# Hand-over from attention to output mix in a decoder layer: chunk 0's rows of the 16-step pattern by DMA from SBUF to SBUF, eight DRAM stores moved behind them

## The chip, the cores and the metric

One Trainium2 chip, one of its cores. The metric is the device time of one execution of the whole layer in microseconds (us); lower is better.

## The reference

One decoder layer over 2048 tokens of width 1024. What bears on the change is the attention group: eight heads of 64, three dilated window patterns, joined by their softmax denominators.

```python
DILATED_PATTERNS = ((128, 1), (512, 4), (2048, 16))
def dilated_attention_branch(q, k, v, pos):
    q, k = apply_rotary(q, pos, inv_freq), apply_rotary(k, pos, inv_freq)
    for window, dilation in DILATED_PATTERNS:
        o, lse = dilated_pattern(q, k, v, window, dilation)
        outs.append(o); lses.append(lse)
    w = jax.nn.softmax(jnp.stack(lses, axis=0), axis=0)
    return jnp.sum(w[..., None] * jnp.stack(outs, axis=0), axis=0)

def reference(...):
    h = rms_norm(x, g_pre_mix)
    rq, rk, rv, rg, aq, ak, av = split(h @ w_in)
    ret = retention_branch(rq, rk, rv, rg)          # chunks of 128 tokens, a state from chunk to chunk
    att = dilated_attention_branch(aq, ak, av)
    x = x + rms_norm(concatenate([ret, att]) @ w_out, g_post_mix)
    h = rms_norm(x, g_pre_ffn)
    return x + rms_norm((silu(h @ w_gate) * (h @ w_up)) @ w_down, g_post_ffn)
```

All tensors are float32. In the pattern with dilation 16 the token t belongs to class t mod 16, and each class is one block of 128 queries.

## The kernel before, in words

The program has three stages. `project` makes the projections. `attention` handles the heads in pairs, four **units** (NU = 4), and in each unit 48 **blocks** of 128 queries (NB = 48): blocks 0 to 15 of dilation 1, 16 to 31 of dilation 4, 32 to 47 of dilation 16. The last stage is one block of code in which `mix` (retention, joining of the three patterns, output projection, both norms) runs over 16 chunks of 128 tokens, and `ffn` follows it. Between `attention` and the last stage every engine meets at a barrier: none starts the new stage before all have ended the old one, SyncE (SP) too.

In `attention` VectorE scores and copies, ScalarE takes exponentials, TensorE multiplies and transposes. Four blocks make a **quad**. The result of a block is a row tile `orow[:, j % 16, :]`, 128 queries by 132 numbers: two sums, 2 x 64 output columns, two minima. VectorE's copy on line 853 (`copy_out`) ends a quad and raises `o_copied`. SP then stores each block to `att_out` in DRAM (line 715, 66 KB), with one semaphore of `stored` for each of the 16 places in the ring. DRAM is there because of the regrouping: the tokens of a block of dilation 16 lie 16 apart, and `mix` wants 128 successive tokens with all three patterns in one tile, `att_in[s]`, 128 tokens by 3 patterns by 4 units of 132 numbers.

SP's order is written out by hand. In the last unit, `sync` on line 718 ff. stores blocks 0 to 43 as they come, and between them `early_sync` issues loads that `mix` needs first; at block 32 it waits on the 16 `stored` semaphores for what the first three units stored, and loads columns 0 to 395 of `att_in[0]` (line 1170). The last four stores stand at the head of the next stage's SP program (`store_last`), followed by two small constants (line 1206), a wait on the 16 semaphores for all stores, and then:

```python
sp.dma_start(att_in[0][:, :, LAST_UNIT:], att_rows(0)[:, :, LAST_UNIT:]).then_inc(att_loaded[0], 16)   # L1209
load_att(sp, 1, 1)                                                                                # L1143
```

In `mix`, chunk 0 runs so. TensorE turns k (line 1298) and scores (line 1306), VectorE applies decays (lines 1386, 1392), TensorE multiplies (lines 1268, 1272) and forms the chunk's key-value products (line 1282, semaphore `kv_done`). VectorE, after the decays, waits for `att_in[0]` in `lowest_parts` (line 1361), forms the weights of the patterns (to line 1380; ScalarE's exponential on line 1489 in between), masks the key-value products (line 1400, which also waits for `kv_done`), sums a variance (lines 1410, 1412), makes the scores of chunk 1, adds the three weighted parts, and scales the retention output (line 1439). TensorE then turns chunk 0 (line 1250), goes through chunk 1's products, and begins the first dense matmuls of the output projection (line 1345). GpSimd (POOL) weights the parts (line 1539) and takes the roots. The same tile's second copy, `att_in[1]`, is read by VectorE for chunk 1 at its second visit to line 1361.

Of the kernel before, what the change touches and what calls it, by code (L numbers as in the profile page):

```python
# [14 lines left out]
P = 128  # L15
# [17 lines left out]
PATTERNS = (1, 4, 16)  # L33
# [613 lines left out]
def attention(nc, D, bank, first, mixed):  # L647
# [5 lines left out]
    NB = len(blocks)  # L653
# [62 lines left out]

    def store_last(sp):

        for j in range(NB - QUAD, NB):
            store_copied(sp, NU - 1, j)  # L720

    def sync(sp):
        def store(u, j):
            sp.wait_ge(o_copied, NB // QUAD * u + j // QUAD + 1)
            store_copied(sp, u, j)

        def unit(u, s, more=True):

            sp.wait_ge(permuted, BY_16 * u + C_PERMUTED)
            sp.sem_inc(waited, 1)  # L730
            sp.wait_ge(scored, NB * u + C_SCORED)
            sp.sem_inc(waited, 1)
            for j in range(NB):
                if more or j < NB - QUAD:
                    store(u, j)
                if more:
                    for n in range(2 * QK_DMAS):
                        if (n // 2 if n < QK_DMAS else QK_DMAS // 2 + 5 * (n - QK_DMAS) // 2) == j:
                            load_qk(sp, D, first, u + 1, 1 - s, n)
                if more and j and j % 4 == 0:  # L740
                    load_values(sp, D, first, u + 1, j // 4 - 1)
                if not more:
                    mixed["early_sync"](sp, j, permuted, BY_16 * NU + C_PERMUTED, [(sem, 16 * ((NU - 1) * NB // RING) + 16) for sem in stored])
            if more:
                load_values(sp, D, first, u + 1, VALUE_LOADS - 1)

        for r, free in enumerate(first["row_free"]):
            sp.wait_ge(free, first["rows_stored"])
        with sp.Fori(0, NU // 2 - 1) as it:
            unit(2 * it, 0)  # L750
            unit(2 * it + 1, 1)
        unit(NU - 2, 0)
        unit(NU - 1, 1, more=False)

# [172 lines left out]
    with nc.Block() as block:  # L927
# [18 lines left out]
        def _(pool):  # L946
            gpsimd(pool)
            mixed["early_gpsimd"](pool)
    mixed["store_last"] = store_last
    mixed["rows_stored"] = [(sem, 16 * (NU * NB // RING) + 16) for sem in stored]  # L950
    spent = [sem for sem in m.given if sem not in stored]
    return spent + [consts, qk_first, qk_rest] + v_loaded + first["row_free"]
# [13 lines left out]
def mix(nc, D, ident, bank):  # L966
# [61 lines left out]
             "h2_done h_turned h_copied").split()  # L1028
    S = {n: m.sem(n) for n in names}
    qkv_loaded, att_loaded = m.sems("qkv_loaded", 2), m.sems("att_loaded", 2)  # L1030
    x_loaded = m.sems("x_loaded", 2)
    x1_stored, h_stored = m.sem("x1_stored"), m.sem("h_stored")
    late_consts, gains_loaded, w_loaded = m.sem("late_consts"), m.sem("gains_loaded"), m.sem("w_loaded")
# [105 lines left out]
    def att_rows(c):  # L1139
        return D["att_out"][:, bass.ts(c, P), :].rearrange("a t n -> t a n")  # L1140
# [5 lines left out]
        src = D["projT"][RG:RG + WIDTH, bass.ts(c, P)].rearrange("(k p) t -> p k t", p=P)  # L1146
        sp.dma_start(gate[:, s], src).then_inc(att_loaded[s], 16)

    def early_sync(sp, j, permuted, all_permuted, rows_stored):

        if j in (1, 4, 7, 10):
            k = 2 * (j // 3)
# [14 lines left out]
        if j == 32:  # L1167
            for sem, count in rows_stored:
                sp.wait_ge(sem, count)
            sp.dma_start(att_in[0][:, :, 0:LAST_UNIT], att_rows(0)[:, :, 0:LAST_UNIT]).then_inc(S["consts"], 16)  # L1170

    def early_vector(dve, j, permuted, all_permuted):

# [25 lines left out]
    def sync(sp, fed):  # L1199
# [1 line left out]

            sp.sem_inc(S["waited"], 1)

        bounds["store_last"](sp)
        for tile, name in ((head_cols, "head_cols"), (chunk_decay, "chunk_decay")):
            sp.dma_start(tile[:], D[name]).then_inc(late_consts, 16)
        for sem, count in bounds["rows_stored"]:
            sp.wait_ge(sem, count)
        sp.dma_start(att_in[0][:, :, LAST_UNIT:], att_rows(0)[:, :, LAST_UNIT:]).then_inc(att_loaded[0], 16)  # L1209
        load_att(sp, 1, 1)  # L1210
        sp.dma_start(gain_mix[:], D["g_post_mix"].broadcast_to([P, DM])).then_inc(gains_loaded, 16)
        sp.dma_start(gain_ffn[:], D["g_pre_ffn"].broadcast_to([P, DM])).then_inc(gains_loaded, 16)
# [139 lines left out]
    def vector(dve, fed):  # L1352
        dve.wait_ge(S["consts"], 16 * CONSTS)

        def step(c, s, on):
            def lowest_parts():
                a = att_in[s][:].rearrange("p a (u n) -> p a u n", n=AO_W)
                lowest = a[:, :, :, 2 * (ATT_D + 1):AO_W]
                three = lambda t: t[:].rearrange("p a (u h) -> p a u h", h=2)
                wait_loaded(dve, att_loaded[s], c, s, 2)  # L1360
                nc.vector.tensor_reduce(att_low[:].rearrange("p (u h) -> p u h", h=2), lowest.rearrange("p a u h -> p u h a"),
                                        AX.X, ALU.min).then_inc(S["maxed"], 1)
                dve.wait_ge(S["maxed"], c + 1)
                if later(c):
                    dve.wait_ge(S["parted"], 3 * c)
                least = att_low[:].rearrange("p (u h) -> p u h", h=2).unsqueeze(1).broadcast_to([P, 3, 4, 2])
                nc.vector.tensor_tensor(three(weight), lowest, least, ALU.subtract).then_inc(S["differed"], 1)
# [146 lines left out]
    def gpsimd(pool):  # L1514
# [6 lines left out]
        def step(c, s, on):  # L1521
# [31 lines left out]
        steps(pool, step)  # L1553

    bounds.update({"sync": sync, "tensor": tensor, "vector": vector, "scalar": scalar, "gpsimd": gpsimd, "sems": S, "early_gpsimd": early_gpsimd,
            "early_sync": early_sync, "early_vector": early_vector, "store_x1": store_x1, "store_h": store_h, "turn_h": turn_h, "make_x1": make_x1, "make_h2": make_h2,
            "square_y": square_y, "square_x": square_x, "copy_h": copy_h, "root_y": root_y, "root_x": root_x,
            "x1_stored": x1_stored, "h_stored": h_stored})
    return bounds
# [1076 lines left out]
```

## Time and profile before

| | |
|---|---|
| runs | 2401.86, 2406.1, 2407.64 us; median 2406.1 |
| profiled execution | 2404.06 us, its span 2402.2 us |
| TensorE busy | 2352.5 us, 98% of the span |
| VectorE, ScalarE, GpSimd busy | 62%, 38%, 25% |
| mean granted TensorE clock | 0.994 of full |

Times below are microseconds from the span's start. A row of the timeline gives start, duration, engine, line, operation, output and input tiles, how many instructions are merged into it, and in brackets how long the engine stood idle before it and what ended that. SPq are SP's instructions that issue DMAs; their duration is that of the issue, not of the transfer. Matmul ends are modelled, so neighbouring rows can overlap a little. A merged row ends at its start plus its duration.

### The profile page before, as it was taken

How to read it: one execution, taken by the hardware profiler on the slowest of the kernel's cores; microseconds unless marked ns; L12 is line 12 of the kernel's file. 1: busy time of each engine (PE TensorE's matmuls, PEld its weight loads, DVE VectorE, ACT ScalarE, POOL GpSimd, SP SyncE). 2: the span in 40 equal slices, each digit the busy share in tenths (PEclk: the TensorE clock that was granted, in tenths of full speed). 3: DMA queues.
4: the chain of work that ended last, by engine and by line, in shares of the span. 5: the costliest groups of instructions: out<-in, count | busy, mean ns of one | idle time of the engine just before them, and what ended most of it. 6: DMA issues, size and time to landing. Idle time of an engine off the chain costs nothing. (4 is left out here: it accounts for less than half of the span.)

```text
span 2402.2 us, 36587 instructions
## 1 busy us (share of the span) xinstructions
PE 2352.5 (98%) x12624; PEld 1968.4 (82%) x12624; DVE 1484.5 (62%) x2769; ACT 917.2 (38%) x1982; POOL 597.7 (25%) x387
## 2 busy tenths in 40 slices
PE   7999999999999899999999999999999999999998
PEld 6888888888889778887888888878888888888887
DVE  4322346645888878789765666876565654456655
ACT  4301122216878623335433333533333343323332
POOL 0089555535544556662000000000000000000001
PEclk9999999999999989999999999999999999999999
DMA  5323214457777555665433333343333336445655
GB/s 180 126 83 110 75 61 122 130 141 183 186 178 195 165 176 183 187 187 197 144 109 92 105 96 115 117 136 101 107 109 93 103 121 219 145 154 193 232 197 191
DMA packets 309294, 344.96 MB, mean 144 GB/s; under 512 B 17088, under 2 KB 240704, under 8 KB 308928
## 3 DMA queue, kind: packets, MB, share of 16 engines
q1 hardware_dynamic: 309184, 343.54, 46.9%
q8 instruction: 63, 1.03, 0.2%
q14 instruction: 47, 0.39, 0.1%
HBM read 231.41 MB, written 112.07 MB: 143 GB/s over the span
## 5 line engine op out<-in xcount | busy, mean ns | idle before, releaser
L1874 PE MATMUL fin_psum_bank<-ff_b_hi,ff_w_hi 128*128 128x512 f32 x1232 | 481.4, 391 | 8.1 <-ACT ff_taken L2015 5.0
L1874 PE MATMUL fin_psum_bank<-ff_b_lo,ff_w_hi 128*128 128x512 f32 x1232 | 479.9, 390 | 0.0
L1874 PE MATMUL fin_psum_bank<-ff_b_hi,ff_w_lo 128*128 128x512 f32 x1232 | 479.8, 389 | 0.0
L2193 POOL TENSOR_TENSOR ff_ssq<-ff_ssq,ff_minus_half 128x1 f32<-128x1 f32 x16 | 14.8, 928 | 1247.5 <-DVE ff_ssq L2485 1247.5
L1874 PEld LDWEIGHTS fin_psum_bank<-ff_b_hi,ff_w_hi 128*128 128x128 f32 x1232 | 231.6, 188 | 60.2 <-ACT ff_taken L2015 7.0
L1874 PEld LDWEIGHTS fin_psum_bank<-ff_b_hi,ff_w_lo 128*128 128x128 f32 x1232 | 231.6, 188 | 48.4
L1874 PEld LDWEIGHTS fin_psum_bank<-ff_b_lo,ff_w_hi 128*128 128x128 f32 x1232 | 231.7, 188 | 47.5
L1956 PE MATMUL fin_psum_bank<-ff_down_hi,ff_act_hi 128*128 128x512 f32 x616 | 239.8, 389 | 0.5 <-DVE ff_act_lo L2225 0.5
L1956 PE MATMUL fin_psum_bank<-ff_down_hi,ff_act_lo 128*128 128x512 f32 x616 | 239.6, 389 | 0.0
L1956 PE MATMUL fin_psum_bank<-ff_down_lo,ff_act_hi 128*128 128x512 f32 x616 | 239.6, 389 | 0.0
L2197 DVE TENSOR_TENSOR ff_w_lo<-ff_raw,ff_w_hi 128x512 fp32r<-128x512 f32 x176 | 120.8, 687 | 140.2 <-ACT ff_w_hi L1967 140.2
L460 PE MATMUL pr_psum_acc<-pr_hT_hi,pr_w_hi 128*128 128x512 f32 x512 | 199.2, 389 | 0.0
L460 PE MATMUL pr_psum_acc<-pr_hT_lo,pr_w_hi 128*128 128x512 f32 x512 | 199.2, 389 | 0.0
L460 PE MATMUL pr_psum_acc<-pr_hT_hi,pr_w_lo 128*128 128x512 f32 x512 | 199.2, 389 | 0.0
L894 ACT ACTIVATE at_prob<-at_prob,at_orow 128x256 f32<-128x256 f32 (+1 forms) x384 | 173.0, 453 | 56.1 <-DVE at_orow L865 55.5
L2015 ACT ACTIVATE ff_taken<-fin_psum_bank 128x512 f32<-128x512 f32 x132 | 78.8, 597 | 222.9 <-PE fin_psum_bank L1874 219.7
L1987 ACT ACTIVATE ff_act_hi<-ff_act_raw 128x1408 fp32r<-128x1408 f32 x56 | 77.4, 1381 | 204.2 <-DMA ff_act_raw<-a_parts 204.1
L1967 ACT ACTIVATE ff_w_hi<-ff_raw 128x512 fp32r<-128x512 f32 x176 | 109.7, 626 | 105.9 <-PE fin_psum_bank L1874 100.3
L2197 DVE TENSOR_TENSOR ff_w_lo<-ff_sums,ff_w_hi 128x512 fp32r<-128x512 f32 x132 | 90.3, 689 | 88.8 <-ACT ff_w_hi L1967 88.8
L865 DVE CUSTOM_DVE_ANT_0 at_prob<-fin_psum_bank,mask 128x256 f32<-128x256 f32 (+1 forms) x384 | 117.2, 359 | 36.4 <-PE fin_psum_bank L777 34.6
L2225 DVE TENSOR_TENSOR ff_act_lo<-ff_act_raw,ff_act_hi 128x1408 fp32r<-128x1408 f32 x56 | 90.9, 1623 | 75.1 <-ACT ff_act_hi L1987 74.5
L1956 PEld LDWEIGHTS fin_psum_bank<-ff_down_hi,ff_act_hi 128*128 128x128 f32 x616 | 115.6, 188 | 24.8 <-DVE ff_act_lo L2225 0.9
(212 smaller groups left out, 4630.5 us busy)
## 6 DMA issues: line engine op xcount, KB each, us to landing
ff_act_raw<-a_parts SPq DMA_DIRECT2D x56, 704.0 KB, 4.1
ff_raw<-in_w_gate SPq DMA_DIRECT2D x22, 1024.0 KB, 5.9
ff_raw<-in_w_up SPq DMA_DIRECT2D x22, 1024.0 KB, 5.3
a_parts<-ff_a_sum SPq DMA_DIRECT2D x88, 256.0 KB, 6.0
ff_down_raw<-in_w_down SPq DMA_DIRECT2D x77, 256.0 KB, 4.6
a_parts<-ff_up SPq DMA_DIRECT2D x66, 256.0 KB, 2.3
att_out<-at_orow SPq DMA_DIRECT2D x192, 66.0 KB, 3.7
vblk<-v_att SPq DMA_DIRECT2D x48, 256.0 KB, 4.8
```

What stands on the lines that cost most here:

```text
L460: last = nc.tensor.matmul(acc[:, g, :], w[s][:, k, :], h[:, k, t], start=k == 0 and n == 0, stop=k == KT - 1 and n == 2)
L865: last = nc.vector.tensor_tensor_reduce(out=prob[:, n % 4, h, keys[j]], in0=s_ps[:, n % NS, h, keys[j]], in1=mask[:, keys[j]], scale=-SCAL ...
L894: last = nc.scalar.activation(pr, pr, ACT.Exp, bias=orow[:, n % RING, LEAST + h:LEAST + h + 1], scale=-1.0, accum_out=orow[:, n % RING, SU ...
L1874: last = nc.tensor.matmul(to, w[:, i, k, :], b[i][:, k, :], start=fresh and k == 0 and which == 0, stop=k == KH - 1 and which == 2, skip_g ...
L1956: last = nc.tensor.matmul(bank[:, ORDER[n], :], a[t % 3][:, k, :], w[o % 2][k][:], start=k == 0 and which == 0, stop=k == PAIRS - 1 and wh ...
L1967: nc.scalar.activation(w_hi[:, i], weight(i, s), ACT.Copy).then_inc(w_hi_done[i], 1)
L1987: nc.scalar.activation(act_hi[t % 3][:], act_raw[t % 3][:], ACT.Copy).then_inc(act_hi_done, 1)
L2015: nc.scalar.activation(taken[:, i, :], X[s], ACT.Copy).then_inc(snapped, 1)
L2193: nc.gpsimd.tensor_tensor(ssq[:, n % 2, 1:2], ssq[:, n % 2, 1:2], minus_half[:], ALU.pow).then_inc(rooted, 1)
L2197: nc.vector.tensor_tensor(w_lo[:, i], weight(i, s), w_hi[:, i].bitcast(F32), ALU.subtract).then_inc(w_lo_done[i], 1)
L2225: nc.vector.tensor_tensor(act_lo[t % 3][:], act_raw[t % 3][:], act_hi[t % 3][:].bitcast(F32), ALU.subtract).then_inc(act_lo_done, 1)
```

## The change

For the last unit alone, the 16 blocks of dilation 16 get a second way out. The tokens of chunk 0 are the first eight rows of each of these row tiles, and SP sends them straight to `att_in[0]` by a DMA from SBUF to SBUF, 8 rows of 132 numbers (4 KB), to every 16th partition. Twelve of these stand in the attention's SP program behind the stores of blocks 32 to 43's places, four at the head of the next stage. The other two patterns of chunk 0's last unit are loaded from DRAM at block 38, after a wait on the 16 `stored` semaphores for blocks 0 to 31. The DRAM stores of blocks 40 to 43 leave the attention's program; eight stores, blocks 40 to 47, now stand in the next stage behind the straight ones and the two constants. The load on line 1209 is gone. VectorE waits once more, for `far_loaded`.

```diff
     def store_last(sp):
 
+        for j in range(NB - 2 * QUAD, NB):
+            store_copied(sp, NU - 1, j)
+
+    def straight(sp, j):
+        far = PATTERNS[-1]
+        mixed["far_rows"](sp, j - (NB - far), far, orow[0:P // far, j % RING, :])
+
+    def straight_last(sp):
         for j in range(NB - QUAD, NB):
-            store_copied(sp, NU - 1, j)
+            straight(sp, j)
...
-                if more or j < NB - QUAD:
+                if more or j < NB - 2 * QUAD:
                     store(u, j)
+                elif j < NB - QUAD:
+                    sp.wait_ge(o_copied, NB // QUAD * u + j // QUAD + 1)
...
                 if not more:
-                    mixed["early_sync"](sp, j, permuted, BY_16 * NU + C_PERMUTED, [(sem, 16 * ((NU - 1) * NB // RING) + 16) for sem in stored])
+                    if NB - PATTERNS[-1] <= j < NB - QUAD:
+                        straight(sp, j)
+                    mixed["early_sync"](sp, j, permuted, BY_16 * NU + C_PERMUTED,
+                                        *([(sem, 16 * (NU * NB // RING - back) + 16) for sem in stored] for back in (3, 1)))
...
+    def far_rows(sp, r, far, rows):
+        sp.dma_start(att_in[0][r:P:far, 2, LAST_UNIT:], rows).then_inc(far_loaded, 16)
...
+        if j == 38:
+            for sem, count in near_stored:
+                sp.wait_ge(sem, count)
+            sp.dma_start(att_in[0][:, 0:2, LAST_UNIT:], att_rows(0)[:, 0:2, LAST_UNIT:]).then_inc(att_loaded[0], 16)
...
-        bounds["store_last"](sp)
+        bounds["straight_last"](sp)
         for tile, name in ((head_cols, "head_cols"), (chunk_decay, "chunk_decay")):
             sp.dma_start(tile[:], D[name]).then_inc(late_consts, 16)
+        bounds["store_last"](sp)
         for sem, count in bounds["rows_stored"]:
             sp.wait_ge(sem, count)
-        sp.dma_start(att_in[0][:, :, LAST_UNIT:], att_rows(0)[:, :, LAST_UNIT:]).then_inc(att_loaded[0], 16)
         load_att(sp, 1, 1)
...
                 wait_loaded(dve, att_loaded[s], c, s, 2)
+                if not later(c):
+                    dve.wait_ge(far_loaded, 16 * PATTERNS[-1])
```

SP's program around the end of the attention, before. The branches are the end of the attention's code and the way into the next stage, the barrier between them; `x11` means eleven in a row:

```order
L1170 DMA mx_att_in_3172<-att_out 128x3x396
L715 DMA att_out<-at_orow 128x132 x11
L927 UNCONDITIONAL_BRANCH
L2565 UNCONDITIONAL_BRANCH
L715 DMA att_out<-at_orow 128x132 x4
L1206 DMA mx_head_cols<-const_head_cols 128x256
L1206 DMA mx_chunk_decay<-const_chunk_decay 128x2
L1209 DMA mx_att_in_3172<-att_out 128x3x132
L1143 DMA mx_att_in_3173<-att_out 128x3x528
```

The same engine and place after the change, the part ahead of the barrier from block 36 on (blocks 32 to 35 alternate in the same way; block 32's straight DMA stands just ahead of the load of 128x3x396):

```order
L1164 DMA mx_att_in_3172<-at_orow 8x132
L715 DMA att_out<-at_orow 128x132
L1164 DMA mx_att_in_3172<-at_orow 8x132
L1191 DMA mx_att_in_3172<-att_out 128x2x132
L715 DMA att_out<-at_orow 128x132
L1164 DMA mx_att_in_3172<-at_orow 8x132 x5
L940 UNCONDITIONAL_BRANCH
L2588 UNCONDITIONAL_BRANCH
```

Between the load at block 32 and the barrier SP issued 11 DMAs, and now 19, with one more ahead of that load.

Behind the barrier, after the change:

```order
L1164 DMA mx_att_in_3172<-at_orow 8x132 x4
L1227 DMA mx_head_cols<-const_head_cols 128x256
L1227 DMA mx_chunk_decay<-const_chunk_decay 128x2
L715 DMA att_out<-at_orow 128x132 x8
L1157 DMA mx_att_in_3173<-att_out 128x3x528
```

The load of 128x3x132 is gone, and `att_in[1]` (here 3173) stands behind eight stores where four stood. On the other four engines the instructions and their order are the same; VectorE has one more wait.

## Rows read from the trace of the kernel before

**Rows 1.** The page: busy time of each engine and share of the span
```profile
PE 2352.5 (98%) x12624; PEld 1968.4 (82%) x12624; DVE 1484.5 (62%) x2769; ACT 917.2 (38%) x1982; POOL 597.7 (25%) x387
```

**Rows 2.** Busy time by stretch: length, then each engine, granted clock, DMA share, GB/s
```profile
836.04:838.80 2.76, 1.91 (x22) 1.51 (x23) 1.71 (x3) 0.00 (x0) 0.00 (x0) 0.94 0.22 59
838.80:862.20 23.40, 17.96 (x119) 15.20 (x119) 13.94 (x31) 2.75 (x6) 13.30 (x12) 0.50 0.65 206
862.20:1090.00 227.80, 227.80 (x1573) 191.81 (x1573) 181.45 (x323) 70.62 (x146) 142.06 (x120) 1.00 0.59 187
```

**Rows 3.** Timeline of TensorE, from the barrier to the dense matmuls
```profile
836.08 0.41 PE L1298 MATMUL fin_psum_bank<-at_ident,mx_qkv 128*128 128x128 f32 x2 [1.05 <-PEq L927]
...
837.96 0.76 PE L1268 MATMUL fin_psum_bank<-mx_state,mx_q_dec 128*128 128x256 f32 x2 [0.81 <-DVE mx_probT L1392]
...
840.11 1.17 PE L1268 MATMUL fin_psum_bank<-mx_state,mx_q_dec 128*128 128x256 f32 x2
...
842.80 0.66 PE L1282 MATMUL fin_psum_bank<-mx_qkv,mx_k_dec 128*32 128x64 f32 x16
...
850.48 1.12 PE L1250 MATMUL fin_psum_bank<-at_ident,mx_ret 128*128 128x128 f32 x4 [3.73 <-DVE mx_ret L1439]
...
860.12 0.80 PE L1345 MATMUL fin_psum_bank<-mx_w_hi,mx_mT_hi 128*128 128x512 f32 x1
```

**Rows 4.** Timeline of VectorE, the same stretch
```profile
835.07 0.69 DVE L853 COPY at_orow<-fin_psum_bank 128x512 f32<-128x512 f32 x1 [0.75 <-PE fin_psum_bank L814]
...
843.20 0.18 DVE L1361 TENSOR_REDUCE mx_att_low<-mx_att_in 128x8 f32<-128x24 f32 x1 [4.70 <-DMA mx_att_in<-att_out]
...
844.68 0.68 DVE L1400 TENSOR_TENSOR mx_kv<-fin_psum_bank,mx_head_cols 128x512 f32<-128x512 f32 x1
...
849.74 0.68 DVE L1439 TENSOR_TENSOR mx_ret<-fin_psum_bank,mx_stat 128x512 f32<-128x512 f32 x1
...
851.13 0.18 DVE L1361 TENSOR_REDUCE mx_att_low<-mx_att_in 128x8 f32<-128x24 f32 x1
...
858.11 0.69 DVE L1400 TENSOR_TENSOR mx_kv<-fin_psum_bank,mx_head_cols 128x512 f32<-128x512 f32 x1 [2.76 <-PE fin_psum_bank L1282]
```

**Rows 5.** Timeline of SP's DMA issues, read in short windows, up to the barrier
```profile
825.92 0.44 SPq L715 DMA_DIRECT2D att_out<-at_orow  x1
826.90 0.39 SPq L1170 DMA_DIRECT2D mx_att_in<-att_out  x1
...
828.34 0.44 SPq L715 DMA_DIRECT2D att_out<-at_orow  x1
830.25 0.33 SPq L715 DMA_DIRECT2D att_out<-at_orow  x1
...
831.58 0.63 SPq L715 DMA_DIRECT2D att_out<-at_orow  x1
833.24 0.33 SPq L715 DMA_DIRECT2D att_out<-at_orow  x1
...
834.09 0.91 SPq L715 DMA_DIRECT2D att_out<-at_orow  x2
```

**Rows 6.** The same view, behind the barrier
```profile
836.04 1.51 SPq L715 DMA_DIRECT2D att_out<-at_orow  x2
...
838.33 0.43 SPq L715 DMA_DIRECT2D att_out<-at_orow  x1
...
840.56 0.38 SPq L1209 DMA_DIRECT2D mx_att_in<-att_out  x1
841.00 0.47 SPq L1143 DMA_DIRECT2D mx_att_in<-att_out  x1
```

**Rows 7.** DMA issues, KB each, us to landing: last store, second constant, att_in[1]
```profile
att_out<-at_orow SPq DMA_DIRECT2D x1, 66.0 KB, 1.7
...
mx_chunk_decay<-const_chunk_decay SPq DMA_DIRECT2D x1, 1.0 KB, 2.0
...
mx_att_in<-att_out SPq DMA_DIRECT2D x1, 792.0 KB, 4.8
```

More of the change, by code:

```diff
@@ L948, in _ @@
             mixed["early_gpsimd"](pool)
-    mixed["store_last"] = store_last
+    mixed["store_last"], mixed["straight_last"] = store_last, straight_last
     mixed["rows_stored"] = [(sem, 16 * (NU * NB // RING) + 16) for sem in stored]
@@ L1030, in mix @@
     qkv_loaded, att_loaded = m.sems("qkv_loaded", 2), m.sems("att_loaded", 2)
+    far_loaded = m.sem("far_loaded")
     x_loaded = m.sems("x_loaded", 2)
@@ L1147, in load_gate, with early_sync @@
         sp.dma_start(gate[:, s], src).then_inc(att_loaded[s], 16)
-    def early_sync(sp, j, permuted, all_permuted, rows_stored):
+    def far_rows(sp, r, far, rows):
+        sp.dma_start(att_in[0][r:P:far, 2, LAST_UNIT:], rows).then_inc(far_loaded, 16)
+    def early_sync(sp, j, permuted, all_permuted, rows_stored, near_stored):
         if j in (1, 4, 7, 10):
@@ L1555, in mix @@
     bounds.update({"sync": sync, "tensor": tensor, "vector": vector, "scalar": scalar, "gpsimd": gpsimd, "sems": S, "early_gpsimd": early_gpsimd,
-            "early_sync": early_sync, "early_vector": early_vector, "store_x1": store_x1, "store_h": store_h, "turn_h": turn_h, "make_x1": make_x1, "make_h2": make_h2,
+            "early_sync": early_sync, "far_rows": far_rows, "early_vector": early_vector, "store_x1": store_x1, "store_h": store_h, "turn_h": turn_h, "make_x1": make_x1, "make_h2": make_h2,
             "square_y": square_y, "square_x": square_x, "copy_h": copy_h, "root_y": root_y, "root_x": root_x,
```

## The prediction

> **What bounds the kernel now.** I read the page first: TensorE is busy 2352.5 us, 98% of the span [rows 1]. So only a stretch in which TensorE stands idle, or runs at the lower clock, can give anything. The busy time by stretch finds the place the change touches: from the barrier at 836.04 to 862.20 TensorE has gaps, and from 838.80 on its granted clock is 0.50 (1.2 GHz instead of 2.4); from 862.20 to 1090 it is busy for 227.80 of 227.80 us at full clock [rows 2]. Whatever moves the start of the dense matmuls (860.12 [rows 3]) thus moves all behind it by as much, and nothing later in the mix stage takes it back.
>
> Next, the timelines, backwards from there. TensorE's longest gap, 3.73 us, ends with the retention output (L1439), after which it runs from 850.48 almost without a stop [rows 3]. VectorE reaches L1439 at 849.74, and from 844.68, where it masks the key-value products (L1400), it goes through without a wait. Ahead of that it stood idle 4.70 us for a DMA, `att_in[0]`, until 843.20, and L1400 came right behind the weights made from it [rows 4]. That wait is what the change removes. But L1400 has a second condition: TensorE's products (L1282), which start at 842.80 and take 0.66 us, so end at 843.46 [rows 3]. So even if `att_in[0]` costs nothing, L1400 can come at most 844.68 - 843.46 = 1.2 us earlier. That is 0.05% of the time: the ceiling, not the forecast.
>
> **The change, part by part.**
>
> *The removed wait.* Before, SP's last store is issued at 838.33 and lands 1.7 us after its issue [rows 7], the load of chunk 0's last columns goes out at 840.56 and VectorE starts at 843.20 [rows 4, 6]: 7.16 us after the barrier's 836.04. Now the last straight DMA takes the last store's place, 2.29 us behind the barrier (838.33 - 836.04). Its landing isn't in this trace; the nearest rows are 1.7 us for a 66 KB store and 2.0 us for a 1 KB load into SBUF [rows 7]. I take 2.0, counted from the issue's end (0.43 us), and 0.1 for the wake: VectorE could start 4.8 us after the barrier and be through with the weights 1.5 us later (844.68 - 843.20), at barrier + 6.3. L1282 ends at barrier + 7.4 (843.46 - 836.04). TensorE's products decide, with 1.1 us to spare.
>
> *What it adds ahead of the barrier.* All engines wait there for SP too. SP's last issue of the old stage ends at 834.09 + 0.91 = 835.00 [rows 5]; VectorE's last copy ends at 835.07 + 0.69 = 835.76, and the first instruction behind the barrier starts at 836.04 [rows 4, 6], 0.28 us later. SP has 0.76 us to spare at the end, and two pauses for `o_copied` on the way: 828.78 to 830.25 (1.47 us) and 832.21 to 833.24 (1.03 us) [rows 5]. The price of one more issue is read there too: four in 833.24 to 835.00 are 0.44 us each, gap included. For a DMA of eight rows I take the same 0.44, since the 1 KB constant and the 66 KB store behind the barrier cost SP alike. The bounds are 0.37 (the shortest issue, 0.33, and a gap of 0.04) and 0.67 (the longest here, 0.63, and the gap) [rows 5]. A wait on 16 semaphores, all long raised, costs SP 826.90 - 826.36 = 0.54 us before the load at block 32 [rows 5], 0.50 more than a plain gap; the change has a second such wait at block 38. Then:
> - up to block 36: four more issues (straight 32 to 35), 1.76 - 1.47 = 0.29 us late;
> - up to block 40: four straight ones, one load and the wait, 5 x 0.44 + 0.50 = 2.70; 0.29 + 2.70 - 1.03 = 1.96 us late;
> - blocks 40 to 43: four straight ones where four stores stood, nothing.
>
> SP arrives at 836.96 instead of 835.00, 1.20 us behind VectorE, so **the barrier opens 1.2 us later**. With 0.37 it is 0.6 us, with 0.67 3.3 us. The cover that hid SP's issues, VectorE's last copies, is used up.
>
> The Trainium skill (DMA: Bandwidth & Descriptors, section Anatomy of one DMA) puts a DMA's dispatch by the sequencer at about 50 ns and nearly all the rest into the landing. By that SP would not be late at all. It describes another issuing path than SP's; the issues in this trace, 0.33 to 0.63 us, speak against it here, so it is a rival and not the sum.
>
> *Behind the barrier.* TensorE's chunk 0 starts 1.2 us later and L1282 ends at 844.66. It also meets the lower clock sooner: at full clock the first product on L1268 took 0.76 us and the second, at half, 1.17 [rows 3]. If the clock falls at 838.8 as before, the first now runs at half as well, + 0.4 us. L1400 then starts at 845.1 against 844.68: **+0.4 us**. `att_in[0]` is ready for it: 837.24 + 6.3 = 843.5. The rest of VectorE's way to L1439 is its own work, so TensorE's L1250 comes 0.4 us later, and so does the dense part. GpSimd gets its weights earlier and waits for nobody new.
>
> *The eight stores moved back.* `att_in[1]` was issued at 841.00 and lands 4.8 us later [rows 6, 7]; VectorE wants it at 851.13 [rows 4]. Now, ahead of it, stand four straight DMAs and two constants as four stores and two constants did, then eight stores, 8 x 0.44 = 3.5 us, less the load that is gone (0.44), and the barrier's 1.2: it goes out at 841.00 + 4.3 = 845.3, and up to 1 us later where the last store's landing must be waited out, and lands at 850.1 to 851.1. That is just in time, and VectorE has 2.76 us of idle time before the next L1400, at 858.11, for which it waits on TensorE [rows 4]. Cost: nothing; if the cover goes, each microsecond past about 854 costs one.
>
> *The rest.* The near load and its semaphores are done long before use; the extra wait of VectorE on `far_loaded` costs some hundredths. GpSimd's first q product waits for the 396-column load, which goes out 0.44 us later; TensorE needs it only at 837.96.
>
> **Sum**: -1.2 at most for the removed wait; +1.2 for the later barrier, +0.4 for the clock: +0.4 us. Against the profiled execution's 2404.06 us that is 2404.5. The median of the runs shown is 2406.1, 2.0 above this execution, so 2406.5 on that scale. The runs shown lie from 2401.86 to 2407.64, so about 0.3% (7.2 us) is what can be told from no change.
>
> **Rivals.**
> - *Small DMAs are cheap to issue.* Under about 0.26 us each (5 x 0.26 + 0.50 - 1.03 = 0.77) SP is not late, the barrier stays, and the ceiling is reached: -1.2 us, 2404.9 on the median's scale. For it: they carry 1/16 of the rows. Against it: 1 KB and 66 KB cost SP alike. It is also what follows from the skill's 50 ns.
> - *SP is late by more, or the second tile is (slower).* SP has single issues of 0.63 us, and two issues behind the barrier took 1.51 us together [rows 6]. It decides from 0.44 us per issue on: with nine more issues in the way, each further 0.1 us adds 0.9 us to the barrier; at 0.67 it opens 3.3 us later, and with the clock's 0.4 that is 3.3 + 0.4 - 1.2 = +2.5 us, 2408.6. If also `att_in[1]` lands past 854, another 1 to 2 us: 2410.
> - *The clock.* 17.96 us of TensorE's work lies in the half-clock stretch of 23.40 us [rows 2]. Should the clock not fall, the work from 850.48 to 862.20 would halve, -5.9 us, with some 2 us ahead of it: -8 us, 2398. Against it: the change makes TensorE's gap ahead of the barrier longer, not shorter. The other way, the clock comes back later: each microsecond more at half costs half a one; a few of them make +2 us, 2408.5.
>   The Trainium skill (TensorE: Matmul & The Clock Gate, section Part 1) says that idleness lowers the clock and sustained activity releases it. By that the longer gap could bring the fall to before 837.2, which slows L1298 and L1306 too: about +0.8 us more than my sum.
> - *It doesn't do what it says*: VectorE still waits long for `att_in[0]`, because 16 little pieces queue on few DMA engines. It decides from a landing 1.1 us later than I take it; +1 us.
>
> **How the numbers follow.** Chances: forecast (-0.5 to +1.5 us) 0.50; cheap issue 0.20; SP or the second tile late 0.17; clock kept 0.03, clock later 0.07; late pieces 0.03. All but the kept clock, and a sum of several of the late ones, lie inside 0.3%. So faster by over 0.3%: 0.04; within: 0.92; slower: 0.04. The range takes the mechanisms from -1.2 to +2.5 us around 2406.1 and, since a median of few runs can itself sit some 2 us off, the edges 2402.0 and 2410.0.
>
> **What would show it.** Right: in the changed profile SP's last issue ahead of the barrier ends near 837, and the first instructions behind it start near 837.2; VectorE's 4.70 us wait at L1361 shrinks to some 2 us (from decays that end 1.2 to 1.6 us later to a landing near 842); L1400 is released by TensorE's L1282; the dense matmuls begin at 860.5, give or take 1. Wrong: the barrier still opens at 836.0 (issues cheaper than read), or L1361's second visit has an idle time of over 2 us, or the half-clock stretch is gone or differs from 23.4 us by several microseconds, or a difference behind 1090, where the change does nothing.

## The result, and the profile after

The changed kernel takes 2408.07 us (median of 20 runs, 2403.85 to 2410.78); the kernel before, now with 20 runs, 2403.06 us (2401.12 to 2408.6). The ratio is 1.0015, 95% interval 1.0009 to 1.0020: **slower by 3.6 us (2.2 to 4.8)**, inside the 0.3% that was called no change, but clear of zero. (The two medians lie 5.0 us apart; the ratio is formed from all runs, whose means lie 3.7 us apart.) A second measurement gave 1.0012 (1.0003 to 1.0022). The profiled execution took 2408.69 us, its span 2406.8.

In this execution the attention ends 1.19 us later than in the one of before, so I count from the end of VectorE's last copy in the attention (835.76 before [rows 4], 836.26 + 0.69 = 836.95 after). Busy time by stretch, columns as in [rows 2], then the page's line of engines, as in [rows 1]:

```profile
836.04:838.80 2.76, 0.19 (x2) 0.00 (x0) 0.69 (x1) 0.00 (x0) 0.00 (x0) 0.81 0.30 76
838.80:862.20 23.40, 14.22 (x92) 12.11 (x93) 12.38 (x29) 2.27 (x5) 7.69 (x8) 0.51 0.45 141
862.20:1090.00 227.80, 226.59 (x1588) 190.28 (x1587) 181.32 (x321) 69.21 (x143) 145.14 (x121) 1.00 0.61 189
```

```profile
PE 2351.2 (98%) x12624; PEld 1968.5 (82%) x12624; DVE 1485.5 (62%) x2769; ACT 917.1 (38%) x1982; POOL 598.1 (25%) x387
```

TensorE does as much as before; it does 3.7 us less of it between 838.80 and 862.20, and nearly nothing between 836.04 and 838.80, where it was busy 1.91 us before. The timeline of TensorE, answering to [rows 3] (line numbers have moved: 1298, 1268, 1282, 1250 and 1345 of before are 1319, 1289, 1303, 1271 and 1366):

```profile
835.57 0.66 PE L827 MATMUL fin_psum_bank<-at_ident,at_oT 128*128 128x128 f32 x4 [0.86 <-DVE at_oT L861]
843.02 0.66 PE L1319 MATMUL fin_psum_bank<-at_ident,mx_qkv 128*128 128x128 f32 x2 [6.79 <-PEq L940]
843.61 1.24 PE L1327 MATMUL fin_psum_bank<-mx_qkv 32*128 32x128 f32 x16
845.66 1.22 PE L1289 MATMUL fin_psum_bank<-mx_state,mx_q_dec 128*128 128x256 f32 x2 [0.81 <-DVE mx_probT L1415]
...
850.97 0.66 PE L1303 MATMUL fin_psum_bank<-mx_qkv,mx_k_dec 128*32 128x64 f32 x16
...
857.63 1.12 PE L1271 MATMUL fin_psum_bank<-at_ident,mx_ret 128*128 128x128 f32 x4 [3.79 <-DVE mx_ret L1462]
...
865.18 0.50 PE L1366 MATMUL fin_psum_bank<-mx_w_hi,mx_mT_hi 128*128 128x512 f32 x1
```

The gap at the barrier, 1.05 us before, is 6.79 us (L940 is the branch at the barrier). The reason is SP. Its timeline, answering to [rows 5, 6]:

```profile
827.77 0.71 SPq L1164 DMA_DIRECT2D mx_att_in<-at_orow  x1
829.03 0.39 SPq L1187 DMA_DIRECT2D mx_att_in<-att_out  x1
829.47 0.48 SPq L715 DMA_DIRECT2D att_out<-at_orow  x1
829.99 0.62 SPq L1164 DMA_DIRECT2D mx_att_in<-at_orow  x1
...
835.62 0.59 SPq L1164 DMA_DIRECT2D mx_att_in<-at_orow  x1
837.15 0.39 SPq L1191 DMA_DIRECT2D mx_att_in<-att_out  x1
837.60 1.56 SPq L715 DMA_DIRECT2D att_out<-at_orow  x1
...
841.66 0.56 SPq L1164 DMA_DIRECT2D mx_att_in<-at_orow  x1
842.99 0.56 SPq L1164 DMA_DIRECT2D mx_att_in<-at_orow  x1
```

A straight DMA holds SP for 0.56 to 0.62 us (0.71 the first), and the next issue starts 0.61 to 0.67 us after its start, where most stores take 0.44 + 0.04. SP no longer pauses, and ends its last issue ahead of the barrier at 841.66 + 0.56 = 842.22, 5.27 us behind VectorE. VectorE, answering to [rows 4]:

```profile
836.26 0.69 DVE L866 COPY at_orow<-fin_psum_bank 128x512 f32<-128x512 f32 x1 [0.75 <-PE fin_psum_bank L827]
...
846.55 0.18 DVE L1384 TENSOR_REDUCE mx_att_low<-mx_att_in 128x8 f32<-128x24 f32 x1 [0.34 <-DMA mx_att_in<-at_orow]
...
851.76 0.69 DVE L1423 TENSOR_TENSOR mx_kv<-fin_psum_bank,mx_head_cols 128x512 f32<-128x512 f32 x1 [3.65 <-PE fin_psum_bank L1303]
...
858.28 0.18 DVE L1384 TENSOR_REDUCE mx_att_low<-mx_att_in 128x8 f32<-128x24 f32 x1
```

The wait that the change was to remove is gone: 4.70 us became 0.34. Nothing is won by it, because the masking (L1423) now stands 3.65 us for TensorE's products. Those are late by the barrier, and in this execution they run at half clock from the start: from TensorE's first instruction behind the barrier to the end of L1303 it takes 8.61 us (843.02 to 851.63), where it took 7.38 before (836.08 to 843.46). These 1.2 us are as much as the change could have won there.

### The profile page after: what moved, and what is told of

Read it like the earlier page. It is cut to its first block and busy times, and to the rows that moved or that the text cites. A ratio compares the mean times of both kernels' runs of the same rounds, so it can differ in the third digit from the quotient of the medians.

```text
span 2406.8 us, 36612 instructions
## 1 busy us (share of the span) xinstructions
PE 2351.2 (98%) x12624; PEld 1968.5 (82%) x12624; DVE 1485.5 (62%) x2769; ACT 917.1 (38%) x1982; POOL 598.1 (25%) x387
```

## The experiments

Each row is one profile; the ratios are to the kernel before, timed in the same rounds on the same chip. The three right-hand columns count from the end of VectorE's last copy in the attention to the first instruction of TensorE behind the barrier, to the masking of chunk 0's products, and to TensorE's turn of chunk 0 (L1250 of before).

| kernel | ratio, 95% interval | barrier | masking | turn of chunk 0 |
|---|---|---|---|---|
| before | 1 | 0.32 | 8.92 | 14.72 |
| before, with the probes at its end | none taken | 0.32 | 8.48 | 14.28 |
| changed | 1.0015 (1.0009 to 1.0020) | 6.07 | 14.81 | 20.68 |
| changed, again | 1.0012 (1.0003 to 1.0022) | 5.81 | 14.56 | 20.43 |
| 12 spare DMAs, 8 rows | 1.0024 (1.0015 to 1.0033) | 6.07 | 14.81 | 20.70 |
| 12 spare, 16 rows | 1.0028 (1.0019 to 1.0037) | 7.14 | 15.89 | 21.86 |
| 12 spare, 8 rows, to DRAM | 1.0007 (0.9998 to 1.0016) | 1.91 | 10.25 | 15.75 |
| 6 spare, 8 rows | 1.0000 (0.9991 to 1.0009) | 1.33 | 9.63 | 15.43 |
| stores 40 to 43 back | 1.0025 (1.0015 to 1.0035) | 7.79 | 16.54 | 22.41 |
| all straight behind | 1.0013 (1.0004 to 1.0021) | 0.33 | 12.83 | 18.63 |
| cut by row | 0.9995 (0.9986 to 1.0003) | 0.32 | 8.53 | 14.33 |
| near load, block 38 | 0.9994 (0.9985 to 1.0003) | 0.32 | 7.73 | 13.52 |
| near load, block 39 | 0.9998 (0.9989 to 1.0007) | 0.32 | 8.30 | 13.71 |
| the same, again | 0.9996 (0.9987 to 1.0005) | 0.33 | 7.90 | 13.70 |

The second row is the probe run described next. Its program is the kernel before up to the last store, so it is a second execution of the same code in this place (its one run, 2446.27 us, holds the probes). VectorE's last copy and masking there, then TensorE's turn of chunk 0:

```profile
835.88 0.69 DVE L853 COPY at_orow<-fin_psum_bank 128x512 f32<-128x512 f32 x1 [0.75 <-PE fin_psum_bank L814]
...
845.05 0.68 DVE L1400 TENSOR_TENSOR mx_kv<-fin_psum_bank,mx_head_cols 128x512 f32<-128x512 f32 x1
```

```profile
850.85 1.12 PE L1250 MATMUL fin_psum_bank<-at_ident,mx_ret 128*128 128x128 f32 x4 [3.73 <-DVE mx_ret L1439]
```

The same code thus differs by 0.44 us between two executions, and a difference of that size in one trace shows nothing.

**What an issue costs, in quiet.** Behind everything else in the kernel before, probe DMAs between row tiles that are done with:

```diff
         sp.wait_ge(out_stored, 16 * CHUNKS)
+        for i in range(6):
+            sp.dma_start(near[2][i:P:16, 0:W], src[0:8, 0:W]).then_inc(probe, 16)
+        sp.wait_ge(probe, 192)
...
```

> The kernel before with probe DMAs behind everything else, when all outputs are stored and all queues are quiet: batches of six issued in a row (8 rows of 528 bytes SBUF to SBUF; the same to every 16th partition; 16 rows; 128 rows; 8 rows to DRAM; 128 rows to DRAM), then single ones of 8 rows and 128 rows to SBUF and 128 rows to DRAM, each waited for. Only the probe's rows are read. Theory A (a DMA of eight rows costs SP more to issue, by its shape): 8 rows start 0.61 us apart here too, 16 and 128 rows 0.45 to 0.48. Theory B (the issues in the changed kernel were slow because the queues were busy): all six kinds start 0.44 to 0.48 us apart. Theory C (SBUF to SBUF is what costs): 8, 16 and 128 rows to SBUF all 0.61, to DRAM 0.45. Round trip of a single 8-row DMA into SBUF: 1.7 to 2.4 us.

SP's timeline: L1873 and L1876 are 8 rows to SBUF (to successive and to every 16th partition), L1879 16 rows, L1882 128 rows, L1885 and L1888 8 and 128 rows to DRAM; from L1891 on single ones, each waited for, 8 rows and 128 rows to SBUF and 128 rows to DRAM:

```profile
2400.99 4.19 SPq L1873 DMA_DIRECT2D ff_near<-ff_near  x6
2406.29 3.63 SPq L1876 DMA_DIRECT2D ff_near<-ff_near  x6
2411.03 3.72 SPq L1879 DMA_DIRECT2D ff_near<-ff_near  x6
2415.97 3.75 SPq L1882 DMA_DIRECT2D ff_near<-ff_near  x6
2421.12 2.00 SPq L1885 DMA_DIRECT2D att_out<-ff_near  x6
2424.07 2.73 SPq L1888 DMA_DIRECT2D att_out<-ff_near  x6
2428.10 4.24 SPq L1891 DMA_DIRECT2D ff_near<-ff_near  x3
2433.44 4.26 SPq L1894 DMA_DIRECT2D ff_near<-ff_near  x3
2439.09 3.60 SPq L1897 DMA_DIRECT2D att_out<-ff_near  x3
```

Six in a row take 3.63, 3.72 and 3.75 us for 8, 16 and 128 rows to SBUF, so 0.60 to 0.63 us each, whatever the rows (0.70 in the first batch, of which one took 0.81 and the others 0.62 to 0.66); to DRAM 0.33 us each with 8 rows and 0.46 with 128. Theory C holds: out of SBUF into SBUF is what costs. Theory A's reason (few rows) and theory B (busy queues) fall. A single DMA, from its issue to the next one, takes 1.81 us to SBUF with 8 rows ((4.24 - 0.62) / 2, the last issue being 0.62 us), 1.90 with 128 rows ((4.26 - 0.46) / 2), and 1.63 with 128 rows to DRAM.

**Only the issues, nothing else of the change.**

```diff
                 if not more:
+                    if NB - 16 <= j < NB - QUAD:
+                        mixed["spare_rows"](sp, j - (NB - 16), orow[0:8, j % RING, :])
...
+    def spare_rows(sp, r, rows):
+        sp.dma_start(spare[r % 16:P:16, r // 16, :], rows).then_inc(spared, 16)
...
```

VectorE's first visit to `att_in[0]` waits for these DMAs too.

> The kernel before, with nothing of the hand-over changed, but twelve DMAs of 8 rows from the row tiles of blocks 32 to 43 to a spare tile, at the places of the twelve straight ones. Theory A (SP's issue time ahead of the barrier is the cause): 12 x 0.63 = 7.6 us more of SP's time, 2.5 us of pauses and 0.76 of slack take up 3.3, the barrier opens 4.3 to 4.8 us later, the dense matmuls start near 864.5 to 865, and since these then fall into full clock about 1 us comes back: +3.3 to +4 us in all. Rival (the stores moved behind the barrier, or the wait on far pieces, is the cause): the barrier opens under 2 us later and the time is at most 1 us longer.

SP's timeline in this kernel, last spare issue and the four stores behind the barrier:

```profile
840.15 0.59 SPq L1153 DMA_DIRECT2D mx_spare<-at_orow  x1
841.49 1.76 SPq L715 DMA_DIRECT2D att_out<-at_orow  x4
```

VectorE's last copy in the same kernel, and TensorE's first instruction behind the barrier:

```profile
834.77 0.69 DVE L855 COPY at_orow<-fin_psum_bank 128x512 f32<-128x512 f32 x1 [0.75 <-PE fin_psum_bank L816]
```

```profile
841.53 0.66 PE L1304 MATMUL fin_psum_bank<-at_ident,mx_qkv 128*128 128x128 f32 x2 [6.80 <-PEq L929]
```

VectorE ends at 835.46, SP at 840.74, TensorE starts at 841.53: barrier, masking and turn lie where the changed kernel has them, with all twelve stores in their old places and the old load of `att_in[0]`. So SP's issue time ahead of the barrier is enough to make the loss. That the two agree to 0.02 us is chance: where this kernel has four more stores (1.9 us), the changed one has the near load with its wait (1.4 us) and a longer single store (1.56 us, here 1.19). The barrier is 5.75 us later and not 4.3 to 4.8; the time is +5.8 us (3.6 to 7.9), above the expected 3.3 to 4, which the interval still touches.

> The same with 16 rows in each of the twelve spare DMAs, twice the bytes. Theory A (eight rows cost more than sixteen to issue): 0.46 to 0.48 us each, 5.7 us in all, the barrier opens 2.4 to 2.9 us later, +1.5 to +2 us in all. Theory C (SBUF to SBUF costs): as with 8 rows, barrier 4.3 to 4.8 us later, +3.3 to +4 us.

The edit is `orow[0:16, ...]`, to every 8th partition. It came out against theory A's first form: 6.8 us later at the barrier, not 2.4 to 2.9, and also more than theory C's 4.3 to 4.8. The spare ones take 0.50 us, but the stores between them 0.58 instead of 0.44, so that a spare DMA and a store together take 1.17 us against 1.11 with 8 rows; one store takes 1.73 us. Why the price moves over to the neighbour is open.

> Six spare DMAs of 8 rows (blocks 32, 34, to 42) instead of twelve, beside the kernel before. Theory A (SP's issue time, with 1.47 and 1.03 us of pauses and 0.76 us of slack as cover): 6 x 0.63 = 3.8 us, 2 x 0.63 inside the first pause, 0.23 over the second, 1.26 more: SP 0.7 us behind VectorE, first instruction behind the barrier 1.2 to 1.6 us after VectorE's last copy against 0.3 before and 6.1 with twelve. Time +0.5 to +1.5 us. Rival (each piece costs in proportion, through the DMA queues): half of twelve's, about 3 us at the barrier, +2.5 to +3 us.

Every second spare DMA is left out. The barrier opens 1.33 us behind VectorE, not 3: the pauses and the slack cover the first six but for 1.0 us, the next six cost 4.7 us. That is a threshold, not a proportion. The ratio is 1.0000 (an interval of 2 us to either side), where +0.5 to +1.5 us was expected.

> Twelve DMAs of the same 8 rows at the same places, but into a scratch tensor in DRAM. Theory C (SBUF as the target of a DMA out of SBUF costs, not the number or the size): 0.33 us each as in the probe, 4.0 us in all, of which 3.3 are covered: barrier 1.2 to 1.8 us behind VectorE's last copy, time +0.5 to +1.5 us. Theory A' (number of DMAs decides, 0.61 each whatever the target): barrier at 6.1 as with the SBUF target, +5 us.

The target is `D["scratch"][r]`, the rest as with twelve. SP's timeline, again the last spare issue and the four stores behind the barrier:

```profile
837.99 0.47 SPq L1153 DMA_DIRECT2D scratch<-at_orow  x1
839.12 2.32 SPq L715 DMA_DIRECT2D att_out<-at_orow  x4
```

TensorE's timeline, first instruction behind the barrier:

```profile
839.15 0.41 PE L1304 MATMUL fin_psum_bank<-at_ident,mx_qkv 128*128 128x128 f32 x2 [2.64 <-PEq L929]
```

1.91 us (1.2 to 1.8 expected) against 6.07 with the same number, rows and places. Theory C again, in the kernel itself. A spare DMA and the store behind it take 0.76 us together, where they took 1.11: 0.26 of the difference is the spare one, 0.09 the store, which took 0.35 us instead of 0.44.

**The other parts of the change.**

> The changed kernel with the stores of blocks 40 to 43 back in the attention's program, the straight DMAs as they are. Theory A: 4 x 0.48 = 1.9 us more of SP ahead of the barrier: first instruction 8.0 us behind VectorE's last copy against 6.1; time 1 to 2 us above the changed kernel's. Rival (the moved stores were what made the change slow): the time falls back towards that of the kernel before.

`store_last` and the two limits with `2 * QUAD` are as in the kernel before. The barrier opens 7.79 us behind VectorE, 1.7 later than in the changed kernel; the ratio is 1.0025, whose interval overlaps the changed kernel's, so the trace and not the time separates the two. The rival, a time back near that of the kernel before, is out. Moving the four stores was a useful part of the change, and not its cost.

> The changed kernel with all sixteen straight DMAs behind the barrier, none ahead of it; the near load stays ahead. Theory A (issue time of SP, ahead of or behind the barrier): the barrier opens as in the kernel before, within 0.5 us, and att_in[0] is complete at the barrier + 16 x 0.61 + 1.5 = 11.3 us, so VectorE's weights end at + 12.8 instead of + 8.7: L1400's place 4.1 us later than before, the time +2 to +4 us. Rival (the landing of the small pieces is slow): later than that by more than a microsecond.

```diff
     def straight_last(sp):
-        for j in range(NB - QUAD, NB):
+        for j in range(NB - PATTERNS[-1], NB):
             straight(sp, j)
...
-                    if NB - PATTERNS[-1] <= j < NB - QUAD:
-                        straight(sp, j)
```

SP's timeline, the sixteen straight ones behind the barrier:

```profile
836.20 9.86 SPq L1162 DMA_DIRECT2D mx_att_in<-at_orow  x16
```

VectorE's timeline, with both visits to the tile:

```profile
847.24 0.18 DVE L1382 TENSOR_REDUCE mx_att_low<-mx_att_in 128x8 f32<-128x24 f32 x1 [8.60 <-DMA mx_att_in<-at_orow]
...
848.72 0.69 DVE L1421 TENSOR_TENSOR mx_kv<-fin_psum_bank,mx_head_cols 128x512 f32<-128x512 f32 x1
...
856.86 0.19 DVE L1382 TENSOR_REDUCE mx_att_low<-mx_att_in 128x8 f32<-128x24 f32 x1 [1.61 <-DMA mx_att_in<-att_out]
```

As expected: the barrier is on time, `att_in[0]` complete 11.0 us behind it (11.3 expected), the masking 3.9 us later. The last issue ends at 846.06 and VectorE goes on at 847.24, 1.18 us later, so the landing of these pieces is not what costs. Here `att_in[1]` is late as well, by 1.61 us.

> The kernel before with only the near load (two patterns of chunk 0's last unit, 16 semaphore waits ahead of it) brought to block 38; the third pattern is loaded behind the last stores as before. Theory A: 0.44 + 0.50 to 0.94 us more ahead of the barrier, in SP's pause of 1.03 us and slack of 0.76 us; barrier at most 0.3 us later; time within 0.5 us of before. Rival (this wait is what holds SP): barrier later by 1 us or more.

```diff
-                    mixed["early_sync"](sp, j, permuted, BY_16 * NU + C_PERMUTED, [(sem, 16 * ((NU - 1) * NB // RING) + 16) for sem in stored])
+                    mixed["early_sync"](sp, j, permuted, BY_16 * NU + C_PERMUTED, *([(sem, 16 * (NU * NB // RING - back) + 16) for sem in stored] for back in (3, 1)))
...
+        if j == 38:
+            for sem, count in near_stored:
+                sp.wait_ge(sem, count)
+            sp.dma_start(att_in[0][:, 0:2, LAST_UNIT:], att_rows(0)[:, 0:2, LAST_UNIT:]).then_inc(att_loaded[0], 16)
...
-        sp.dma_start(att_in[0][:, :, LAST_UNIT:], att_rows(0)[:, :, LAST_UNIT:]).then_inc(att_loaded[0], 16)
+        sp.dma_start(att_in[0][:, 2, LAST_UNIT:], att_rows(0)[:, 2, LAST_UNIT:]).then_inc(far_loaded, 16)
```

The barrier is not later, as expected, and the time (0.9994) doesn't differ by more than its interval. What I had not expected is the gain: the load behind the stores, a third of the bytes, is issued at 843.29 and VectorE starts at 845.20, 1.91 us later, against 840.56 and 843.20 before [rows 4, 6], 2.64 us. The masking comes 1.2 us earlier behind VectorE's last copy than in the profile before, **as much as the prediction's ceiling, through DRAM and without one straight DMA**. Against the second execution of the kernel before it is 0.75 us (8.48 - 7.73). The shorter landing makes 0.7 of it; the rest is that the load is issued 4.06 us behind SP's first issue behind the barrier where it was 4.52, which the edit doesn't explain. In this profile the clock fell only at 849.26, behind the masking, so TensorE's products ended at 844.37 and held nothing up. SP's timeline, the load behind the stores:

```profile
843.29 0.33 SPq L1214 DMA_DIRECT2D mx_att_in<-att_out  x1
```

VectorE's timeline, the instruction that waited for it:

```profile
845.20 0.18 DVE L1368 TENSOR_REDUCE mx_att_low<-mx_att_in 128x8 f32<-128x24 f32 x1 [3.51 <-DMA mx_att_in<-att_out]
...
846.68 0.68 DVE L1407 TENSOR_TENSOR mx_kv<-fin_psum_bank,mx_head_cols 128x512 f32<-128x512 f32 x1
```

> Another cut of the same copy: behind the barrier eight DMAs, each one partition of all sixteen row tiles to sixteen partitions of att_in[0]; ahead of the barrier only the near load, at block 39; stores of blocks 40 to 43 where they were. Theory A: nothing is late at the barrier (within 0.3 us), eight issues of 0.46 us (16 pieces each, not eight) and 1.5 us to land give att_in[0] at the barrier + 5.2, weights at + 6.7, ahead of TensorE's L1282 at + 7.4; L1400 is released by TensorE, 1.2 us earlier than in the kernel before, dense matmuls at 859 in place of 860.1, time -0.5 to -1.2 us. If these issues cost 0.61 too: att_in[0] at + 6.4, -0.3 to -0.8 us. Rival (the chain has another end I have not seen): no change.

```diff
+    mixed["far_row"] = lambda q: orow[q:q + 1, :, :]
...
-        bounds["store_last"](sp)
+        for q in range(8):
+            sp.dma_start(att_in[0][16 * q:16 * q + 16, 2, LAST_UNIT:], bounds["far_row"](q)).then_inc(far_loaded, 16)
         for tile, name in ((head_cols, "head_cols"), (chunk_decay, "chunk_decay")):
             sp.dma_start(tile[:], D[name]).then_inc(late_consts, 16)
+        bounds["store_last"](sp)
...
```

The eight issues take 5.40 us, 0.68 each on average (seven stand 0.63 to 0.64 us apart from the next, one takes 0.93), also from SBUF to SBUF. `att_in[0]` is there 6.75 us behind the barrier (843.53, SP's first at 836.78; 6.4 expected at 0.61 each), 0.4 us earlier than before. The masking, at 8.53, is 0.4 us earlier than in the profile before but no earlier than in the second execution of the same kernel (8.48), so no gain is shown. By the traces this cut is better than the change and not better than the load from DRAM.

> The kernel before with the near load and its 16 waits at block 39 instead of 38, the third pattern loaded from DRAM behind the last stores; no straight DMA. Counted from the end of VectorE's last copy: barrier at + 0.3 as before; the load behind the stores, now a third of the bytes, lets VectorE start its weights 1.2 us earlier than before (5.9 us behind the barrier, not 7.2), and L1400 falls at + 7.7 instead of + 8.9. Time -0.5 to -1.5 us. Rival (what block 38's version showed came from its clock, which fell late): L1400 at + 8.9 again when the clock falls early.

> The version with the near load at block 39, a second time, because its chain was 1.0 us shorter in the trace and its time not clear of the kernel before. Expected: L1250 13.5 to 13.8 us behind VectorE's last copy again (14.7 before), time -0.5 to -1.5 us; if the two measurements together still include no change, the microsecond is below what such a comparison can tell.

Both traces have the turn of chunk 0 at 13.7 us, 1.0 earlier than in the profile before and 0.6 earlier than in its second execution (14.28). The masking was expected at 7.7. In the first the clock had fallen by 836.9, before TensorE's first product (836.97, which took 1.22 us), and TensorE was the last the masking waited for (8.30); in the second it fell at 840.6 and it was VectorE's own weights (7.90). So the rival is half right: an early fall of the clock takes a part of the gain. VectorE's line from the first of the two:

```profile
843.07 0.69 DVE L1407 TENSOR_TENSOR mx_kv<-fin_psum_bank,mx_head_cols 128x512 f32<-128x512 f32 x1 [0.49 <-PE fin_psum_bank L1287]
```

The time stays unresolved: 0.9994, 0.9998 and 0.9996 over three measurements of the two versions, each interval with 1 in it. Their mean, 0.9996, would be the microsecond of the traces, but it isn't shown. Against the changed kernel, timed in the same rounds in the last two runs, it is 2402.08 against 2406.47 us, 0.9996 against 1.0012; with the first measurement of each (0.9998 and 1.0015) nearly the same difference comes out twice (0.0016 and 0.0017).

> The changed kernel on the same chip as the version above, in the same rounds. Expected: first instruction behind the barrier 6.1 us and L1250 20.7 us behind VectorE's last copy, whether or not the clock falls in the early attention as it did in its first profile; time +3 to +5 us.

The change gives nearly the same chain again (5.81 and 20.43 us; here one store took 1.35 us and not 1.56), and 1.0012, +2.9 us.

## Why the prediction was right or wrong

**What bounds the start of the mix**: right. Barrier, TensorE's products and `att_in[0]` are what the masking waits for in every version.

**The direction, and that it stays under 0.3%**: right, though the sum gave it narrowly. Its +0.4 us was what remained of terms of -1.2, +1.2 and +0.4, and was too small by 3.2. 2408.07 lies in the range, whose upper edge allowed for a median that sits off; the shift itself, 3.6 us, is above the +2.5 us that its mechanisms reached.

**The ceiling of 1.2 us**: right for the execution that it was read from. It hangs on when the clock falls: TensorE's products end 7.70 us behind VectorE's last copy in the profile before, 8.07 in the second execution of the same code. The near load alone gave -1.2, -0.6 and -1.0 us at the masking against the first, and -0.75, -0.2 and -0.6 against the second.

**"For a DMA of eight rows I take the same 0.44"** is the step that failed. The nearest rows were stores to DRAM and a load from DRAM; none went from SBUF to SBUF, which costs 0.61. From the load at block 32 to the end of the last issue ahead of the barrier I had 9.6 us (827.34 to 836.96); it was 13.2 (829.03 to 842.22). Of the 3.6 us between, about 11 x 0.19 = 2.1 are this price (0.63 with the gap, for 0.44), 1.1 one store that took 1.56 us (L715 at 837.60), 0.4 the second wait on 16 semaphores: 836.21 to 837.15, 0.94 us, of which I had 0.54. The issue of block 32's straight DMA, 0.71, added some tenths more. My upper bound, 0.67 per issue, held the price; what I took was the middle of rows of another kind. But the sum for that bound has a fault of its own. It leaves blocks 40 to 43 at "nothing", though at 0.67 four straight DMAs stand where four stores of 0.44 stood, so its 3.3 us should be 4.2. Done so with the measured 0.63, the sum has SP 3.5 us behind VectorE, and with the long store and the longer wait 5.0; measured were 5.27.

**"The barrier opens 1.2 us later"**: 5.75 us. Beside the issues, a barrier for which SP is last opens 0.77 us behind SP's last issue (842.22 to 842.99), and 0.28 behind VectorE where that is last.

**"VectorE could start 4.8 us after the barrier"**: 3.6 (842.99 to 846.55). The landing was no problem; the rival of late pieces is out.

**The eight stores**: right. VectorE's second visit to the tile at 858.28 has no wait.

**The clock**: both its effects are there, both larger than in the sum. It fell ahead of the barrier, as the sentence beside the clock's rival had it, so L1319 and L1327 took 0.66 and 1.24 us (0.41 and 0.73 before, at full clock), and the first L1289 took 1.22 in place of 0.76: together +1.2 us at the end of the products, where the sum had +0.4 and that sentence 0.8 more. That the longer gap brings the fall isn't shown: in versions whose gap stayed 1.05 us it fell from 1.6 us (all straight behind) to 10.3 us (near load, block 38) behind VectorE's last copy.

In this execution the clock also gave something back. The stretch at half clock was 23.9 us long in both profiles, and the dense matmuls began at 865.18 at full clock, where before they began at half. By TensorE's turn two chunks later the 5.96 us had become 3.69 (887.71 - 836.95 against 882.83 - 835.76). TensorE's timeline of the changed kernel, of the kernel before, and of the changed kernel's second profile:

```profile
887.71 0.60 PE L1271 MATMUL fin_psum_bank<-at_ident,mx_ret 128*128 128x128 f32 x4
```

```profile
882.83 0.60 PE L1250 MATMUL fin_psum_bank<-at_ident,mx_ret 128*128 128x128 f32 x4
```

```profile
889.66 0.60 PE L1271 MATMUL fin_psum_bank<-at_ident,mx_ret 128*128 128x128 f32 x4
```

The second profile of the changed kernel gave nothing back: 889.66 - 836.59 is 53.07 us, 6.0 more than before. So the loss at that turn was 3.7 us in one execution and 6.0 in the other. The 3.6 us of the measurement is near the first, but that this is its make-up isn't shown.

**The rivals**: "SP is late by more" is what happened, with 3.3 us at the barrier where 5.75 were measured. "Cheap to issue" is out: the cheapest of 45 probes took 0.29 us, and from SBUF to SBUF none took under 0.46. The Trainium skill (DMA: Bandwidth & Descriptors, section Anatomy of one DMA) gives about 50 ns for the sequencer's dispatch on GpSimd's path. These probes show that the figure doesn't carry over to SP.

## What to carry to other kernels

Ahead of a barrier an issuing queue is an engine like any other: count its instructions, its pauses and its slack, and price each transfer by a row with the same source and target. Past the slack every issue moves all engines: the first six cost 1.0 us at the barrier and nothing that the time resolves, the next six 4.7. Before cutting a bulk load into direct pieces, see whether most of it can simply be issued earlier: here two thirds of the bytes moved ahead took 0.6 to 1.2 us from the chain in the traces, about what sixteen direct copies could at best have taken, though the time doesn't resolve it. And profile the kernel before more than once: its own two executions differ by 0.44 us here, over a third of what the change could win.

## What the runs showed of the hardware

- SP's issue of a DMA costs by its target: out of SBUF, with the queues quiet, 0.60 to 0.63 us to SBUF for 8, 16 and 128 rows of 528 bytes (0.70 in the first batch), to DRAM 0.33 (8 rows) and 0.46 (128 rows).
- In a mix of two kinds the cost can show at the neighbour: stores took 0.44 us between spare DMAs of 8 rows, 0.58 between those of 16 rows, 0.35 between those to DRAM. Not explained.
- In many versions one store takes much longer. The added issues alone don't make it, since the kernel before has one too, behind the barrier, where no engine waits at the barrier for it: 1.13 us, issued 0.67 us behind VectorE's last copy. In the changed kernel's two profiles and the two with 16 rows and with stores back, the long store (1.33 to 1.73 us) starts 0.4 to 0.65 us behind that copy, and now stands ahead of the barrier. With 8 spare rows it was 1.19 us and stood 2.7 us ahead of the copy's end. Not explained. SP's timeline of the kernel before:

```profile
836.43 1.13 SPq L715 DMA_DIRECT2D att_out<-at_orow  x1
```

- A wait on 16 semaphores that are all long raised took SP 0.5 us in most places; at block 38, behind a straight DMA, it took 0.93 to 0.94 us in all three traces that have it.
- The stretch at half clock around the barrier differs from execution to execution by more than the change is worth: 23.9 us in the profiles before and after, 6.8 in the first near-load version, 17.1 in the version at block 39, 17.1 also in the probe run, whose code here is that of the kernel before, 30.7 in the changed kernel's second profile, whose turn of two chunks later (889.66 - 836.59 = 53.1) lay 2.3 us behind the first's (50.8). This is likely a good part of why ten to twenty runs don't resolve one microsecond; that wasn't tested.
